# C attention: transposing the probabilities on VectorE and through a scratch array instead of on TensorE

## The chip, the cores and the metric

The kernel runs on one NeuronCore of a Trainium2 chip. Its engines work side by side and meet at semaphores: TensorE (PE in the profile; its weight loads are PEld), VectorE (DVE), ScalarE (ACT), GpSimd (POOL) and SyncE (SP), which here only issues DMAs. The metric is the device time of one execution in microseconds (us).

## The reference, cut to what matters

Two layers over a sequence of 1024 rows of width 2048, in float32. Each layer projects `x` with `w_in`, runs three mixers on parts of the result, gates them, projects with `w_out`, and normalises. The change touches mixer C alone: eight heads of width 64, in chunks of 64 frames, where each frame sees its own chunk and the eight before.

```python
s = jnp.einsum('bnqhd,bnkhd->bnhqk', qc, kb).astype(jnp.float32) * (C_HEAD_DIM ** -0.5)
s = s + bias[None, None]                       # bias[h, clip(t - s)]
s = jnp.where(valid[None, :, None, None, :], s, NEG_INF)
p = jax.nn.softmax(s, axis=-1)
o = jnp.einsum('bnhqk,bnkhd->bnqhd', p.astype(vb.dtype), vb)
```

The scores come out with the queries on the partitions. The last product needs the probabilities `p` with the keys on the partitions, so they must be transposed.

## The kernel before, in words

The work goes in four **steps** (`it` 0 to 3): two layers, and in each the first and the second half of the sequence, 512 rows. A step is even (first half) or odd (second half). Each step has these parts in this order: four **pairs** of C heads (`pair(p)`, which also hold mixer A), a part for keys and values of B (`KV0`), eight tiles of B (`B0`), and the output projection (`O0`). The layer normalisation of a step (`centre`, `gain_and_bias`, `turn_rows`) is done by VectorE inside the pairs of the next step.

All projections are cut into **units**: 512 columns of 128 weight rows, each worth 12 matmuls of 512 columns (fp32 is split into a high and a low part, and three of the four products are kept). A pair holds 24 units. For each unit SyncE loads `raw` (256 KB, ring of four), ScalarE rounds it to `wh` (L974, `split`), GpSimd subtracts to get `wl` (L1340), and TensorE uses both. ScalarE's split of unit u + 3 stands in its program at `slot(u)` and waits until TensorE is done with unit u - 1; SyncE's load of a unit waits until GpSimd has finished with the unit four before it. So a load is issued about seven units ahead of its use.

Inside a pair the scores are made in four **rounds** j = 0 to 3, each for 128 queries of both heads. A round of an odd step sees five blocks of 128 keys (640 columns); a round of an even step sees j + 1 blocks. A round is this chain:

1. `c_scores` (PE): scores into the PSUM bank pair `sc`.
2. `c_max` (DVE, L1422 to L1426): bias added, negated row maximum.
3. `c_exp` (ACT, L1026): exponential into `prob`, with row sums.
4. `c_normalise` (DVE, L1432, L1433): reciprocal, and `prob` times it.
5. `c_transpose` (PE, L681): each 128x128 block by a matmul with the identity, into `sc` again.
6. `c_hi` (ACT) and `c_lo` (DVE, L1373): high and low part of it, from `sc` into `pt`.
7. `c_attend` (PE): values times `pt`, into `pv`. Then `c_low_rows` (ACT) and `c_add` (DVE, L1403, L1406) fold the parts into `c_att`.

Each engine runs its own written order, in which these pieces stand between the units: all four rounds lie between unit 16 and the first unit of the next pair (unit 24), and the chain of one round ends before that of the next is far along. The product with the gate (`attention_product`) and its high and low parts (`mix_hi`, `mix_lo`) close the pair. The pairs are hardware loops (`Fori`) on each engine. The identifiers `tmp`, `values_scratch` and `store_values` belong to the transposing of C's values, which already goes by VectorE's 32x32 transposes and a scratch array in HBM.

Of the kernel before, what the change touches and what calls it, by code (L numbers as in the profile page):

```python
# [54 lines left out]
TWOS = B_TILES // 2  # L55
C_KEYS = 640
# [22 lines left out]
O0 = B0 + B_TILES * U_B  # L79
U_STEP = O0 + 4 * U_N  # L80

# [22 lines left out]
def build(nc, x, x_t, wall, a_gw, a_scale, sinks, rel_rev, ln_gain, ln_bias, rope_cos, rope_sin,  # L104
          pool_coef, pool_inv, out):
    with ExitStack() as ctx:
# [19 lines left out]
        bval_d = nc.dram_tensor("b_values_scratch", (DEPTH, CHUNK + SEQ, P), F32, kind="Internal").ap()  # L126
        tz_d = nc.dram_tensor("bias_rows_scratch", (DEPTH * 8, P * TZ), F32, kind="Internal").ap()
# [20 lines left out]
        bq0 = sb("bq0", [P, CHUNKS, 2, CHUNK], F32R)  # L148
        pt = sb("pt", [P, 5, 2, 2, P], F32R)
# [32 lines left out]


# [58 lines left out]
        c_out = [pv[:, 0:512], pv[:, 512:1024], pv[:, 0:512], sc[0][:, 0:512]]  # L242
# [62 lines left out]
        hist_in = sem("hist_in")  # L305
# [5 lines left out]
        cs_exp = sem("cs_exp")  # L311
        cs_prob = sem("cs_prob")
        ct_full = sem("ct_full")
# [60 lines left out]
        def last_rows(t, a, b):  # L374

            return sums[:, 4 * t:4 * t + 4, :].rearrange("p c n -> p (c n)")[:, a:b]

# [21 lines left out]
        def _(sp):  # L399
# [98 lines left out]
            for it in range(STEPS):  # L498
                with sp.Fori(0, C_PAIRS) as p:
                    for s in range(U_C):  # L500
                        if s == (4 if it else 0):

                            sp.wait_ge(gwl_ok, p + (C_PAIRS * it + 1))
                            sp.dma_start(gw[:], a_gw[layer(it), ds(p, 1)].rearrange("o c d -> (o c) d")
                                         ).then_inc(gw_in, 16)
                        if s == 9 and half(it):

                            sp.wait_ge(w_used, unit(it, p * U_C) + (2 + RING))
                            for m, a, b in ((mixh, 0, 3), (mixl, 3, 6)):
                                sp.dma_start(m[:, MIX_B:MIX_B + 2 * (b - a) - 1:2, :].bitcast(F32),  # L510
                                             hist_d[ds(p, 1), :, a:b, :].rearrange("o p a n -> (o p) a n")
                                             ).then_inc(hist_in, 16)
                        if s == 10:

                            sp.wait_ge(bias_ok, p + (C_PAIRS * it + 1))
                            if it:
                                sp.wait_ge(rope_ok, (B_TILES + 1) * it)
                                sp.wait_ge(bt_full, 2 * B_TILES * it)
                            else:
                                sp.wait_ge(tz_out, p * (16 * DEPTH) + 16 * DEPTH)  # L520
                            sp.dma_start(brope[:, 0, :].rearrange("p (h n) -> p h n", h=2),
                                         tz_d[ds(2 * p + 8 * layer(it), 2), 127:127 + P * (TZ - 1)]
                                         .rearrange("h (q c) -> q h c", c=TZ - 1)[:, :, 0:NEAR]).then_inc(bias_in, 16)
                        if s == 8 and it:

                            sp.wait_ge(w_used, unit(it, p * U_C) + (1 + RING))
                            load_ln(it - 1, p)
                        at = s - (15 if it else 8)
                        if at == 0:
                            store_values(it, p)  # L530
                        if at == 1:
                            load_values(it, p)
                        if s == 20 and it:
                            store_ln(it - 1, p)
                        if s in (21, 22) and turns(it):
                            store_turned(it - 1, p, s - 21)
                            if s == 22:
                                store_turned(it - 1, p, 2)
                        if s == (23 if it else 15) and not half(it):

                            wait_alone(k_ok, p + (C_PAIRS * it + 1))
                            wait_alone(v_ok, p + ((C_PAIRS + 1) * it + 1))
                            for m, a, b in ((mixh, 0, 3), (mixl, 3, 6)):
                                sp.dma_start(hist_d[ds(p, 1), :, a:b, :].rearrange("o p a n -> (o p) a n"),
                                             m[:, MIX_B + 1:MIX_B + 2 * (b - a):2, :].bitcast(F32)).then_inc(hist_out, 16)
# [91 lines left out]
        def _(pe):  # L637
# [98 lines left out]
            for it in range(STEPS):  # L736
# [7 lines left out]
                def pair(p, first=False):  # L744
# [6 lines left out]
                    else:  # L751
                        for s in range(1, 4):
                            quarter(s, 0)
# [1167 lines left out]
```

## Time and profile before

| | |
|---|---|
| median of 3 runs | 2826.12 us (2825.72 to 2827.51) |
| the profiled execution, its own time | 2824.71 us |
| its span in the trace | 2822.9 us |
| granted TensorE clock, mean | 0.999 of full |
| PE, PEld busy | 2807.9 us (99%), 2352.1 us (83%) |
| DVE, ACT, POOL busy | 1762.0 us (62%), 1297.4 us (46%), 1277.3 us (45%) |
| DMA | 384.49 MB, queue q1 44.2% of 16 engines, 311957 packets, of which 129408 under 512 B |

"Busy" is the time in which at least one instruction of the engine runs. Matmuls overlap: one of 512 columns is shown as 390 ns long, and the next starts 0.23 us after it, so the cost of a matmul is read from start to start. An instruction group's line gives busy time and mean length, and behind the bar the engine's idle time before it and what ended that.

### The profile page before, as it was taken

The numbers are of one execution on the slowest core, as the hardware profiler recorded it, in microseconds if no ns is written. First come the engines' busy times: TensorE is split into PE (matmuls) and PEld (weight loads), VectorE is DVE, ScalarE is ACT, GpSimd is POOL, SyncE is SP. The second block draws the span as 40 slices with busy tenths as digits, with TensorE's granted clock in tenths as the row PEclk, the third lists the DMA queues.
The fourth block names the chain that finished last, engine by engine and source line by source line (L and its number), as shares of the span: only waits on it lengthen the run. The fifth ranks groups of instructions, "written<-read, shape, count | busy, mean of one in ns | idle before, by whom it ended". The sixth has DMA issues, their size and how long they took to land.

```text
span 2822.9 us, 45252 instructions
## 1 busy us (share of the span) xinstructions
PE 2807.9 (99%) x13316; PEld 2352.1 (83%) x13316; DVE 1762.0 (62%) x2950; ACT 1297.4 (46%) x2685; POOL 1277.3 (45%) x927
## 2 busy tenths in 40 slices
PE   9999999999999999999999999999999999999998
PEld 7888888888888888888888888888888888888886
DVE  5555679623777777862266666895137766678625
ACT  5444466523444445652244444664235444456521
POOL 4444444444444434444444444444444444444441
PEclk9999999999999999999999999999999999999999
DMA  6444332355555533335565663324564454333442
GB/s 212 132 133 131 100 89 82 112 175 176 169 168 167 162 91 98 86 94 179 172 192 172 174 173 105 86 82 133 155 214 133 129 155 151 100 86 84 136 157 101
DMA packets 311957, 384.49 MB, mean 136 GB/s; under 512 B 129408, under 2 KB 149920, under 8 KB 308128
## 3 DMA queue, kind: packets, MB, share of 16 engines
q1 hardware_dynamic: 308048, 367.26, 44.2%
q10 hardware_dynamic: 3792, 15.73, 1.4%
q8 instruction: 66, 1.08, 0.2%
q14 instruction: 51, 0.42, 0.0%
HBM read 327.23 MB, written 58.81 MB: 137 GB/s over the span
## 4 chain that ended last, share of the span: by engine, by line
PE 99%; DVE 0%; DMA 0%; issue 0%; ACT 0%; POOL 0%; SPq 0%; POOLq 0%
PE acc L639 70%; PE sc L639 18%; PE pv L639 9%; PE sc L681 2%; PE sc L718 1%; DMA raw<-in_wall 0%; DVE last_sums L1840 0%; DVE last_sums L1839 0%; POOL wl L1340 0%; DVE xl L1373 0%; SPq L489 0%; DVE av L1811 0%; DVE last_sums L1820 0%; ACT wh L974 0%; ACT xh L974 0%
## 5 line engine op out<-in xcount | busy, mean ns | idle before, releaser
L1340 POOL TENSOR_TENSOR wl<-raw,wh 128x512 fp32r<-128x512 f32 x920 | 1276.5, 1391 | 1501.9 <-ACT wh L974 1499.9
L974 ACT ACTIVATE wh<-raw 128x512 fp32r<-128x512 f32 x920 | 575.6, 630 | 1053.1 <-PE acc L639 722.3
L639 PE MATMUL acc<-xh,wh 128*128 128x512 f32 x2624 | 1034.0, 394 | 1.2 <-DVE xl L1373 1.2
L639 PE MATMUL acc<-xh,wl 128*128 128x512 f32 x2624 | 1022.7, 390 | 0.0
L639 PE MATMUL acc<-xl,wh 128*128 128x512 f32 x2624 | 1022.6, 390 | 0.0
L639 PEld LDWEIGHTS acc<-xh,wl 128*128 128x128 f32 x2624 | 492.6, 188 | 105.4
L639 PEld LDWEIGHTS acc<-xh,wh 128*128 128x128 f32 x2624 | 493.2, 188 | 98.2 <-DVE xl L1373 2.0
L639 PEld LDWEIGHTS acc<-xl,wh 128*128 128x128 f32 x2624 | 493.6, 188 | 94.0
L1373 DVE TENSOR_TENSOR xl<-prob,xh 128x512 f32 x48 | 55.6, 1158 | 235.8 <-ACT xh L974 235.8
L639 PE MATMUL sc<-wh,mixh 128*128 128x512 f32 x496 | 193.5, 390 | 0.1
L639 PE MATMUL sc<-wl,mixh 128*128 128x512 f32 x496 | 193.0, 389 | 0.0
L639 PE MATMUL sc<-wh,mixl 128*128 128x512 f32 x496 | 193.0, 389 | 0.0
L1373 DVE TENSOR_TENSOR pt<-sc,pt 128x512 fp32r<-128x512 f32 (+3 forms) x192 | 120.1, 663 | 80.7 <-ACT pt L974 79.7
L974 ACT ACTIVATE pt<-sc 128x512 fp32r<-128x512 f32 (+3 forms) x192 | 104.1, 577 | 82.2 <-PE sc L718 43.8
L1026 ACT ACTIVATE prob<-sc,nmax 128x640 f32<-128x640 f32 (+4 forms) x128 | 84.8, 662 | 71.9 <-DVE nmax L1426 70.0
L639 PEld LDWEIGHTS sc<-wh,mixh 128*128 128x128 f32 x496 | 93.1, 188 | 19.6 <-POOL wl L1340 0.5
L639 PEld LDWEIGHTS sc<-wh,mixl 128*128 128x128 f32 x496 | 93.1, 188 | 19.4
L639 PEld LDWEIGHTS sc<-wl,mixh 128*128 128x128 f32 x496 | 93.2, 188 | 19.1
L639 PE MATMUL acc<-wh,mixh 128*128 128x512 f32 x256 | 100.0, 391 | 0.0
L639 PE MATMUL acc<-wh,mixl 128*128 128x512 f32 x256 | 99.7, 389 | 0.0
L639 PE MATMUL acc<-wl,mixh 128*128 128x512 f32 x256 | 99.7, 389 | 0.0
L639 PE MATMUL pv<-wh,mixh 128*128 128x512 f32 x240 | 93.4, 389 | 0.0
(217 smaller groups left out, 3577.4 us busy)
## 6 DMA issues: line engine op xcount, KB each, us to landing
raw<-in_wall SPq DMA_DIRECT2D x920, 256.0 KB, 2.7
res_scratch<-res ACTq DMA_DIRECT2D x12, 1024.0 KB, 4.2
res<-res_scratch SPq DMA_DIRECT2D x12, 1024.0 KB, 4.9
res<-in_x SPq DMA_DIRECT2D x8, 1024.0 KB, 7.3
x_scratch<-res SPq DMA_DIRECT2D x8, 1024.0 KB, 5.2
x_t_scratch<-turned SPq DMA_DIRECT2D x128, 64.0 KB, 2.6
prob<-x_t_scratch SPq DMA_DIRECT2D x32, 256.0 KB, 2.8
res<-x_scratch SPq DMA_DIRECT2D x8, 1024.0 KB, 6.2
```

The source lines that it names most:

```text
L639: return nc.tensor.matmul(o, lhsT, rhs, start=start, stop=stop)
L681: last = nc.tensor.transpose(sc[h][:, cs], prob[:, h, cs], ident[:])
L718: last = nc.tensor.transpose(b_sc[g][:, u, c, :], probs(v, g)[:, u, c, :], ident[:])
L974: return nc.scalar.activation(o, i, ACT.Copy, scale=scale)
L1026: nc.scalar.activation(prob[:, h, c0:C_KEYS], sc[h][:, at:at + C_KEYS - c0], ACT.Exp, bias=nmax[:, h, 0:1], accum_out=psums[:, h, 0:1]).th ...
L1340: nc.gpsimd.tensor_tensor(wl[:, s, :], raw[:, s, :], wh[:, s, :].bitcast(F32), ALU.subtract).then_inc(w_lo, 1)
L1373: return V.tensor_tensor(o, whole, hi.bitcast(F32), ALU.subtract)
```

## The change

The transposing of C's probabilities leaves TensorE. VectorE transposes each 32x32 square of `prob` in place (`V.transpose`), SyncE stores the four bands of 32 rows into `c_prob_scratch` in HBM with the squares put in their new places (four DMAs for each head and round, in pieces of 128 bytes), and loads the transposed blocks back into `pt_raw`, an fp32 view of the place of the low part of `pt` (one DMA for each head and round). `c_hi` and `c_lo` then read `pt_raw` in SBUF instead of `sc` in PSUM. Between the reciprocal and the transpose ScalarE multiplies `prob` by the reciprocal (a `Copy` with a scale), where VectorE did.

The pieces are put in other places of every engine's program. Rounds 0 to 2 get their scores after units 16, 19 and 22, round 3 after unit 1 of the next pair (unit 25); the products with the values come after units 23, 27, 30 and 34. C's closing product (`c_tail_product`, `mix_hi`, `mix_lo`) is between units 11 and 15 of the next pair. The last pair of a step does this in the KV and B parts. `exp` of a round now also waits until the stores of the round before have landed (`cp_out`), since it overwrites `prob`. The load of gain and bias into `prob` waits for the same. The loops over pairs are written out. `hist_in` is split in two, for keys and for values, and the values are loaded later.

```diff
+STORE_AT = (26, 29, 32, 36)
+LOAD_AT = (28, 31, 35, 38)
+ROPE_AT = C_PAIRS * 24 + 11
...
+            def store_c_prob(it, p, j, h):
+                n = c_step(it, p, j)
+                if n:
+                    sp.wait_ge(cp_in[h], 16 * n)
+                sp.wait_ge(cs_prob, 2 * n + h + 1)
+                c0 = 0 if half(it) else 512 - P * j
+                for r in range(4):
+                    rows = slice(32 * r, 32 * (r + 1))
+                    sp.dma_start(cprob_d[h, c0:C_KEYS, rows].rearrange("(m a) b -> a m b", a=32),
+                                 prob[rows, h, c0:C_KEYS].rearrange("a (m b) -> a m b", b=32)).then_inc(cp_out[h], 16)
+
+            def load_c_prob(it, p, j, h):
+                n = c_step(it, p, j)
+                sp.wait_ge(cp_out[h], 64 * (n + 1))
+                if n:
+                    sp.wait_ge(c_pv, n)
+                b0 = 0 if half(it) else 4 - j
+                sp.dma_start(pt_raw[:, b0:5, h, :], cprob_d[h, b0 * P:C_KEYS, :].rearrange("(c k) q -> k c q", k=P)
+                             ).then_inc(cp_in[h], 16)
...
+            def load_gain_bias(it, n):
+                if n:
+                    for h in range(2):
+                        sp.wait_ge(cp_out[h], 64 * c_step(it + 1, n, 0))
...
-            def c_transpose(it, p, j):
-                c0 = 0 if half(it) else 512 - P * j
-                for h in range(2):
-                    pe.wait_ge(cs_prob, p * 8 + (8 * C_PAIRS * it + 2 * j + h + 1))
-                    for b in range(c0 // P, 5):
-                        cs = slice(b * P, (b + 1) * P)
-                        last = nc.tensor.transpose(sc[h][:, cs], prob[:, h, cs], ident[:])
-                    last.then_inc(ct_full, 1)
...
             def c_exp(it, p, j):
...
+                    if n:
+                        act.wait_ge(cp_out[h], 64 * n)
+                    act.wait_ge(cs_max, 2 * n + h + 1)
                     nc.scalar.activation(prob[:, h, c0:C_KEYS], sc[h][:, at:at + C_KEYS - c0], ACT.Exp,
                                          bias=nmax[:, h, 0:1], accum_out=psums[:, h, 0:1]).then_inc(cs_exp, 1)
+                for h in range(2):
+                    act.wait_ge(cs_rinv, 2 * n + h + 1)
+                    copy(prob[:, h, c0:C_KEYS], prob[:, h, c0:C_KEYS], rinv[:, h, 0:1]).then_inc(cs_norm, 1)
...
-                    V_(V.reciprocal(rinv[:, h, 0:1], psums[:, h, 0:1]))
-                    V.tensor_scalar(prob[:, h, c0:C_KEYS], prob[:, h, c0:C_KEYS], rinv[:, h, 0:1], None, ALU.mult
-                                    ).then_inc(cs_prob, 1)
+                    V.reciprocal(rinv[:, h, 0:1], psums[:, h, 0:1]).then_inc(cs_rinv, 1)
+                for h in range(2):
+                    dv.wait_ge(cs_norm, p * 8 + (8 * C_PAIRS * it + 2 * j + h + 1))
+                    V.transpose(prob[:, h, c0:C_KEYS], prob[:, h, c0:C_KEYS]).then_inc(cs_prob, 1)
...
-                    lo(ptl[:, b0:5, h, :], sc[h][:, b0 * P:5 * P].rearrange("p (b q) -> p b q", q=P), pth[:, b0:5, h, :]
-                       ).then_inc(ct_lo, 1)
+                    lo(ptl[:, b0:5, h, :], pt_raw[:, b0:5, h, :], pth[:, b0:5, h, :]).then_inc(ct_lo, 1)
```

On TensorE, an odd step of the kernel before, the end of unit 22 of a pair: the transposes of round 2 stand before mixer A's product (`mixh,bq`), and the scores of round 3 and the values' product of round 2 follow with nothing between them.

```order
L681 MATMUL sc<-ident,prob 128x128 x10
L788 REGISTER_ALU
L639 MATMUL acc<-mixh,bq 128x512
L639 MATMUL acc<-mixl,bq 128x512
...
L639 MATMUL sc<-mixh 128x320 x4
L665 REGISTER_ALU
L639 MATMUL sc<-mixl 128x320 x4
L687 REGISTER_ALU
L639 MATMUL pv<-pt,mixh 128x256 x5
L639 MATMUL pv<-pt,mixl 128x256 x5
```

The same place of the changed kernel, up to the first unit after the next scores:

```order
L699 MATMUL acc<-mixh,bq 128x512
...
L699 MATMUL sc<-mixh 128x320 x4
L699 MATMUL sc<-mixl 128x320 x4
L699 MATMUL acc<-xh,wh 128x512
...
L699 MATMUL pv<-pt,mixh 128x256 x5
L699 MATMUL pv<-pt,mixl 128x256 x5
L699 MATMUL acc<-xh,wh 128x512
...
```

No transposes are left, and one unit's twelve matmuls stand between the scores of round 2 and the values' product, now of round 0.

On VectorE, an odd step of the kernel before, rounds 2 and 3 of a pair:

```order
L1433 TENSOR_SCALAR prob<-prob,rinv 128x640
L1401 REGISTER_ALU
L1403 TENSOR_TENSOR c_low<-pv,c_low 64x512
L1356 REGISTER_ALU
L1406 TENSOR_TENSOR c_att<-c_low 64x128 x2
L1373 TENSOR_TENSOR pt<-sc,pt 128x5x128 x2
L1648 SCALAR_TENSOR_TENSOR tmp<-acc,scale,gate 128x512
L1419 REGISTER_ALU
L1422 MEMSET sc 64x64
```

The same engine in the changed kernel, from `c_lo` of round 0 to `c_lo` of round 1, which is past the end of the pair:

```order
L1455 TENSOR_TENSOR pt<-pt_raw,pt 128x5x128 x2
L1750 SCALAR_TENSOR_TENSOR tmp<-acc,scale,gate 128x512
...
L1518 STREAM_TRANSPOSE prob<-prob 128x640 x2
L1455 TENSOR_TENSOR mixl<-tmp,mixh 128x512
L1485 TENSOR_TENSOR c_low<-pv,c_low 64x512
L1488 TENSOR_TENSOR c_att<-c_low 64x128 x2
L1474 SCALAR_TENSOR_TENSOR gate<-gate,acc 128x512
...
L1509 TENSOR_REDUCE nmax<-sc 128x1
L1455 TENSOR_TENSOR pt<-pt_raw,pt 128x5x128 x2
```

Between the two `c_lo` stand now: A's product, the maxima of round 2 and its transposes, A's low part, a fold, the gate, and the maxima of round 3.

On SyncE, the changed kernel, the end of an odd step's last pair (`raw` are the unit loads):

```order
L430 DMA raw<-in_wall 128x512
L477 DMA c_prob_scratch<-prob 32x20x32 x8
L430 DMA raw<-in_wall 128x512 x3
L487 DMA pt_raw<-c_prob_scratch 128x5x128 x2
L619 DMA brope<-in_rope_cos 128x512
```

Each round puts eight stores and two loads into the queue of the unit loads; the kernel before has none of them.

## Rows read from the trace of the kernel before

**Rows 1.** chain that ended last, of the page: shares of the span by engine.
```profile
PE 99%; DVE 0%; DMA 0%; issue 0%; ACT 0%; POOL 0%; SPq 0%; POOLq 0%
```

**Rows 2.** waits of TensorE over the whole span: us, times, longest.
```profile
PE sc L735 <- POOL ident L1333: 1.6, 1, 1.6
```

**Rows 3.** timeline of TensorE, plain stretch: start us, length us, instruction, count.
```profile
403.25 0.39 PE L639 MATMUL acc<-xh,wh 128*128 128x512 f32 x1
...
405.06 0.39 PE L639 MATMUL acc<-xh,wl 128*128 128x512 f32 x1
```

**Rows 4.** timeline of TensorE, odd step, transposes of five blocks.
```profile
2308.15 1.25 PE L681 MATMUL sc<-ident,prob 128*128 128x128 f32 x10
2309.16 0.48 PE L639 MATMUL acc<-xh,wh 128*128 128x512 f32 x1
...
2310.63 0.76 PE L639 MATMUL sc<-mixh 128*128 128x320 f32 x4
```

**Rows 5.** timeline of TensorE, even step, transposes of one block.
```profile
1606.22 0.38 PE L681 MATMUL sc<-ident,prob 128*128 128x128 f32 x2
1606.36 0.48 PE L639 MATMUL acc<-xh,wh 128*128 128x512 f32 x1
...
1608.50 0.40 PE L639 MATMUL sc<-mixh 128*128 128x256 f32 x2
```

**Rows 6.** instruction group of TensorE: count, busy us, mean ns.
```profile
L681 PE MATMUL sc<-ident,prob 128*128 128x128 f32 x480 | 63.3, 273 | 0.0
```

**Rows 7.** timeline of VectorE, odd step, quarter two.
```profile
2320.57 0.11 DVE L1422 MEMSET sc<- 64x64 f32 x1 [0.38 <-PE sc L639]
...
2322.66 0.82 DVE L1426 TENSOR_REDUCE nmax<-sc 128x1 f32<-128x640 f32 x1
...
2327.50 1.56 DVE L1373 TENSOR_TENSOR pt<-sc,pt 128x640 fp32r<-128x640 f32 x2
2328.97 0.74 DVE L1648 SCALAR_TENSOR_TENSOR tmp<-acc,scale,gate 128x512 f32<-128x512 f32 x1
```

**Rows 8.** timeline of ScalarE, the same stretch.
```profile
2323.55 0.80 ACT L1026 ACTIVATE prob<-sc,nmax 128x640 f32<-128x640 f32 x1
2324.24 0.19 ACT L1026 ACTIVATION_READ_ACCUMULATOR prob<-sc,nmax 128x1 f32 x1
2325.04 0.63 ACT L974 ACTIVATE wh<-raw 128x512 fp32r<-128x512 f32 x1 [0.61 <-PE acc L639]
2326.27 1.30 ACT L974 ACTIVATE pt<-sc 128x640 fp32r<-128x640 f32 x2 [0.60 <-PE sc L681]
```

**Rows 9.** instruction groups of VectorE by form.
```profile
L1373 DVE TENSOR_TENSOR pt<-sc,pt 128x640 fp32r<-128x640 f32 x64 | 49.8, 820 | 26.3 <-ACT pt L974 25.8
L1373 DVE TENSOR_TENSOR mixl<-s,mixh 128x512 fp32r<-128x512 f32 x16 | 20.7, 1294 | 13.2 <-ACT mixh L974 13.1
L1403 DVE TENSOR_TENSOR c_low<-pv,c_low 64x512 f32<-64x512 f32 x48 | 32.6, 679 | 0.5
L1544 DVE STREAM_TRANSPOSE turned<-res 128x512 f32<-128x512 f32 x32 | 19.9, 680 | 0.2
L1406 DVE TENSOR_TENSOR c_att<-c_low 64x128 f32<-64x128 f32 x128 | 71.8, 561 | 3.1
```

**Rows 10.** instruction group of GpSimd, of the page.
```profile
L1340 POOL TENSOR_TENSOR wl<-raw,wh 128x512 fp32r<-128x512 f32 x920 | 1276.5, 1391 | 1501.9 <-ACT wh L974 1499.9
```

**Rows 11.** DMA issues of the page: KB each, median us to landing.
```profile
raw<-in_wall SPq DMA_DIRECT2D x920, 256.0 KB, 2.7
x_t_scratch<-turned SPq DMA_DIRECT2D x128, 64.0 KB, 2.6
```

**Rows 12.** DMAs to the scratch array of values: ns min/median/max, landing.
```profile
L420 SPq DMA_DIRECT2D values_scratch<-tmp x64: 348/355/2172, 37.8 to 2361.4; - x64
DMA to landing us min/median/max: 1.7/2.1/10.0
```

**Rows 13.** busy us of PE, PEld, DVE, ACT, POOL over one odd pair.
```profile
2178.00:2258.30 80.30, 80.30 (x406) 68.29 (x405) 57.04 (x97) 38.29 (x68) 35.72 (x25) 1.00 0.44 141
```

More of the change, by code:

```diff
@@ L79 @@
 O0 = B0 + B_TILES * U_B
+O0_BEGIN = B0 + U_B
 U_STEP = O0 + 4 * U_N
@@ L311, in build @@
         cs_exp = sem("cs_exp")
+        cs_rinv = sem("cs_rinv")
+        cs_norm = sem("cs_norm")
         cs_prob = sem("cs_prob")
-        ct_full = sem("ct_full")
+        cp_out = [sem(f"cp_out{h}") for h in range(2)]
+        cp_in = [sem(f"cp_in{h}") for h in range(2)]
         ct_hi = sem("ct_hi")
@@ L498, in _ @@
             for it in range(STEPS):
[L499 to L545, printed above, removed]
-                        if it == 0:
-                            load_unit(it, p * U_C + (s + FIRST), (s + FIRST) % RING)
-                        else:
-                            load_unit(it, p * U_C + s, s % RING)
-                        if s == 23 and it:
-                            if turns(it):
-                                store_turned(it - 1, p, 3)
-                            wait_alone(ln_out, p * 16 + (64 * (it - 1) + 16))
@@ L751, in pair @@
                     else:
-                        for s in range(1, 4):
-                            quarter(s, 0)
+                        quarter(1, 0)
+                        if p:
+                            c_scores(it, p - 1, 3)
+                        quarter(2, 0)
+                        quarter(3, 0)
+                        if p:
+                            c_attend(it, p - 1, 1)
                         pe.wait_ge(gate_ok, p * 2 + (MIXES * it + 1))
@@ L1112, in pair @@
                     else:
-                        for s in range(2, 5):
-                            slot(s)
+                        slot(2)
+                        if p:
+                            c_hi(it, p - 1, 1)
+                        slot(3)
+                        if p:
+                            c_exp(it, p - 1, 3)
+                        slot(4)
                     used(it, p * U_C + (6 if first else 3))
@@ L1572, in _, with c_tail_product @@
                 pc, nb = C_PAIRS * it, 16 * it
-                per_c = 27 + (2 if it else 0) - half(it)
-                with dv.Fori(0, C_PAIRS) as p:
-                    section(p * per_c + total)
+                def c_tail_product(p, values):
+                    dv.wait_ge(c_fold, c_step(it, p, 3) + 1 + 2)
+                    attention_product(p * 2 + (MIXES * it + 2), values)
+                for p in range(C_PAIRS):
+                    section(total)
+                    if p:
+                        c_max(it, p - 1, 3)
+                        c_lo(it, p - 1, 1)
                     V.tensor_copy(coef1[:], coef[:, ds(p, 1), :].rearrange("p o n -> p (o n)"))
@@ L1660, in _ @@
                     if not half(it):
                         dv.wait_ge(hist_out, p * 32 + (32 * C_PAIRS * layer(it) + 32))
-                    assert count[1] == per_c, (it, count[1])
-                total += C_PAIRS * per_c
+                    total += count[1]
                 section(total)
+                p = C_PAIRS - 1
+                c_max(it, p, 3)
+                c_lo(it, p, 1)
+                c_normalise(it, p, 3)
+                c_add(it, p, 1)
+                c_lo(it, p, 2)
@@ L1667, in _ @@
+                dv.wait_ge(rope_in, 32 * (it + 1))
+                rotate(it, 0, KV0 + 3, 0)
+                c_add(it, p, 2)
+                rotated_query(ROTS * it + 1, 0)
+                rotate(it, 1, KV0 + 7, 1, 1.0)
+                c_lo(it, p, 3)
+                c_add(it, p, 3)
+                c_tail_product(p, C_PAIRS * (it + 1))
                 dv.wait_ge(prod_ok, MIXES * it + 2 * C_PAIRS + 2)
```

288 lines of the change are left out of this document (186 added, 102 removed).

## The prediction

> **What bounds the kernel now.** I read the chain that ended last first: TensorE has 99% of it [rows 1]. Then TensorE's waits: the longest entry of the whole span is 1.6 us, at the start [rows 2]. So TensorE runs without a gap, at full clock (a granted clock of 1.00 in [rows 13]), and the time is the sum of what its instructions cost from start to start. The reader is to see two things in this: anything taken off TensorE is gained in full, and any wait put onto it is lost in full. The other engines have room on average: in an odd pair of 80.3 us VectorE is busy 57.0, ScalarE 38.3, GpSimd 35.7 [rows 13]. Whether they have room at each place is the question of this change.
>
> **What goes.** On a plain stretch nine matmuls start within 1.81 us (403.25 to 405.06), eight intervals, 0.226 us each [rows 3]; a unit of twelve is 2.7 us. The transposes of five blocks and two heads take 2308.15 to 2309.16, 1.01 us; of one block and two heads 1606.22 to 1606.36, 0.14 us [rows 4, 5]. So a further block-and-head costs (1.01 - 0.14) / 8 = 0.109 us. The matmuls behind a run of transposes are late too: six of them take 1.47 us (2309.16 to 2310.63) where 6 x 0.226 is 1.36, and nine take 2.14 (1606.36 to 1608.50) where 2.03 is due, 0.11 us both times. There are 480 transposes [rows 6] in 64 runs (4 steps, 4 pairs, 4 rounds). Sum: 480 x 0.109 = 52.3 us, and 64 x (0.14 - 2 x 0.109 + 0.11) = 2.0 us, together 54.3 us. The busy time of 63.3 us in [rows 6] is not the price, since it counts overlap with the next matmul.
>
> **What TensorE gets.** Scores and values' product were neighbours 48 times and are now apart, each between two projections. A change of form costs at least nothing and at most the 0.11 us seen behind transposes; I take 0.04 us, 2 us in all (0 to 5). The written-out loops cost nothing: TensorE never waited at a loop's end [rows 2], and nothing is added that it must branch for. So without any new wait the profiled time goes from 2824.71 to 2824.7 - 54.3 + 2 = 2772.4 us. The profiled execution is 1.4 us under the median of the runs, and I make the sum against it.
>
> **What the round costs now.** The chain of a round in an odd step, all from rows: maxima of two heads 2.9 us (2320.57 to 2322.66 + 0.82, [rows 7]); the second exponential 0.80 with 0.19 for its sum, a little overlapped, so 0.9 [rows 8]; then new: normalising on ScalarE. No row shows it. Its nearest are the 640-column copies from PSUM, 1.30 for two [rows 8], and the split from SBUF, 0.63 for 512 columns; I take 0.70 each (0.6 to 0.8). The transposes on VectorE: 0.68 us for 128x512 from SBUF to SBUF [rows 9], so 0.85 for 640 columns; the second ends about 0.85 after the second normalise plus a wait for the first. The store: four DMAs of SyncE at 0.355 us each for issuing [rows 12], 2.9 us for two heads, landing 2.6 us after the last of them: 64 KB in 128-byte pieces took a median of 2.6 us, as long as 256 KB of `raw` took in whole rows [rows 11]. Bounds are 1.7 and 10.0 [rows 12]. The load of 320 KB: 2.7 for 256 KB of `raw`, so some 3 to 4 us. From the maxima's end to data in `pt_raw`: 0.9 + 1.4 + 0.9 + 2.9 + 2.6 + 3.5 = 12.2 us, against the 7 to 9 units of 2.7 us (19 to 24 us) that the new places leave between scores and product. The round trip through HBM fits with some 4 us over, after 2.9 us for the maxima.
>
> **What it does to `c_lo`.** Before it read PSUM and took 0.82 us for 640 columns [rows 9]. Now both inputs lie in SBUF. The nearest row is the low part of A's values, 128x512 with both inputs in SBUF: 1.29 us on average [rows 9], near GpSimd's own subtraction of 1.39 [rows 10] rather than near 0.68. So such an instruction often waits for GpSimd's. Bounds for 640 columns are 0.82 and about 1.7; I take 1.15, as GpSimd is busy 35.7 of 80.3 us.
> The Trainium skill ("SBUF — State Buffer", section "SBUF: two separate sides") says why: VectorE with two SBUF inputs and GpSimd share a port pair by an exclusive lock. The trace agrees: 1.29 against 0.68. By that rule the transposes, which have one input, are not held up, and all eight `c_lo` of a pair may be; taken at its worst it gives the second rival below.
>
> **Where it gets tight.** I count from the end of unit 22 in an odd pair, in us. TensorE: scores of round 2 (eight matmuls of 320 columns; by columns and [rows 3] 8 x 0.226 x 320/512 = 1.13, I take 1.25), unit 23, product 0 (ten of 256 columns, 1.13 by the same rule, I take 1.2), unit 24, unit 25, scores 3 (1.25), units 26 and 27: product 1 is due at 17.3. Product 0 is due at 4.0. ScalarE: split 0.63, two `c_hi` 1.4, ready at 2.0. VectorE: `c_lo` 0 ends at 2.9 to 3.8, in time for product 0. Then its queue, in the order shown with the change: A's product 0.74 [rows 7], maxima of round 2 2.9, ending at 6.5 to 7.4; the wait for exponential and normalise and two transposes, to 9.9 to 10.8; A's low part 0.7 to 1.3; the fold, 0.68 and two of 0.29 to 1.3 ([rows 9], mean 0.56; a pair took 1.62 in [rows 7]), the gate, of the same kind as A's product, 0.7: 12.7 to 14.7. Maxima of round 3 (scores are there at 11.9) to 15.6 to 17.6, and `c_lo` 1 to 17.2 to 20.2. Its second half is needed at 17.9. So TensorE waits 0 to 2.3 us there; I take 1.1. There are 8 such places in the two odd steps (three pair boundaries and the KV part, each step): 9 us. Product 3 is due after unit 34, behind `centre`, the transposes of the values and A's low part on VectorE, and its load can only go once product 2 is done (`c_pv`): I take 0.5 us for each of 8 (0 to 1.5), 4 us. At the entry to B, `rotate`, the last folds and the keys' low part now come after C's tail on VectorE: 0.7 us in each step (0 to 2), 3 us. In even steps round 1 has two blocks and round 2 three, every link is shorter, and I take no wait. Together 16 us: 2772.4 + 16 = 2788 us.
>
> **What hides the rest.** A unit's split may be late by three units less split and subtraction, 3 x 2.7 - 0.63 - 1.39 = 6.1 us [rows 3, 8, 10], before TensorE notices. In the odd chain above ScalarE is held for about 4.5 us by the wait for reciprocals; the loads of `raw` are held for 2 to 3 us by ten more issues a round (3.6 us of SyncE) and its waits. Both stay below 6.1, and that is the cover; beyond it each us costs a us. DMA has a mean share of 0.44 in the odd pair [rows 13]; twice 2.6 MB more in 75 us is no new bound, though it makes landings longer.
>
> **Rivals.**
> *No new wait.* If `c_lo` meets GpSimd seldom and folds are short, all lower ends hold: 2772 us. For it: the lower ends above all meet their due times. Against: 32 places must all be in time. Chance 0.2.
> *VectorE late everywhere.* `c_lo`, fold and low parts at their upper ends: 8 x 2.3 + 8 x 1.5 + 4 x 2 = 38 us, 2811 us. For it: 1.29 us against 0.68 for 512 columns [rows 9], and a fold pair of 1.62 [rows 7]. Chance 0.2.
> *The store's landing decides, slower.* `exp` of a round waits until the round before has been stored. In rounds 1 and 3 of an odd pair I find no room there: the store's last DMA is issued about 2.9 us after the transposes and must land within 2.6 us. If a landing in this traffic is 5 to 6 us instead, ScalarE stands with its splits behind it, and the next maxima, `c_lo` and product come about 3 us later, in even pairs as well: 16 x 3.5 + 16 = 72 us, 2844 us. It makes the kernel slower from 52 / 16 = 3.3 us of wait a pair on. For it: landings of up to 10.0 us in [rows 12]; against: medians of 2.1 and 2.6. Chance 0.13.
> The Trainium skill ("DMA: Bandwidth & Descriptors", section "Specifications") speaks for this rival: below 512 bytes a transfer is a read-modify-write and misses line rate, and these pieces are 128 bytes. The trace agrees in part: 64 KB of them take as long as 256 KB in long rows [rows 11]; a wait for it is not in the trace.
> *The removal gives less than it says*, the small switches and waits eat it up to within 0.2%. Chance 0.05.
>
> **How the numbers follow.** My forecast, 2788 us, has 0.42, with its own range of 2779 to 2800. The range given is 2771 to 2822: it takes in the first two rivals and the start of the third, and leaves out the rest of the third. A run tells a difference of 0.2% (5.6 us) from none. Faster by more than that: 0.42 + 0.2 + 0.2 and a little of the third, 0.83. Within it 0.05. Slower 0.12.
>
> **What would show it.** In the changed profile L681's group is gone and the sum of the other TensorE groups is unchanged. TensorE's waits list product 1 of odd steps behind VectorE's `pt` by about 1 us a time, four a step; product 3 and B's first scores behind VectorE by less. `pt` by VectorE takes over 1 us for 640 columns, the transposes of `prob` 0.85, ScalarE's `prob<-prob,rinv` 0.7. The forecast is wrong if unit matmuls wait for GpSimd's `wl` (then a queue was later than 6.1 us), if `exp` waits for the scratch's DMAs by more than 1 us a round, or if even steps wait.

## The result, and the profile after

| | before | after |
|---|---|---|
| median | 2825.96 us (4 runs) | 2915.20 us (4 runs, 2914.46 to 2916.40) |
| the profiled execution's own time, span | 2824.71, 2822.9 us | 2914.46, 2912.4 us |
| granted TensorE clock, mean | 0.999 | 0.984 |

The changed kernel takes 1.0315 of the time before, interval 1.0297 to 1.0333: 89 us slower, where the prediction had 2788 us and a range up to 2822.

The page of the changed kernel: the busy times, what DMA moved, and the chain that ended last by engine.

```profile
PE 2797.6 (96%) x12836; PEld 2323.0 (80%) x12836; DVE 1805.2 (62%) x2950; ACT 1350.6 (46%) x2804; POOL 1276.2 (44%) x927
DMA packets 629705, 448.10 MB, mean 154 GB/s; under 512 B 385664, under 2 KB 467616, under 8 KB 625824
PE 73%; DMA 8%; DVE 8%; SPq 6%; issue 3%; ACT 1%; POOL 1%; ACTq 0%; POOLq 0%; DVEq 0%
```

TensorE lost its 480 transposes (13316 matmuls became 12836) and is no longer the whole chain as in [rows 1]: 22% of it now lies with DMA, VectorE and SyncE's queue. The packets have doubled, and four in five of the added ones are below 512 bytes. TensorE's waits, us in total, times, longest, against [rows 2], where the longest entry is 1.6 us:

```profile
PE pv L699 <- DVE pt L1455: 73.1, 36, 7.6
PE sc L699 <- DVE tmp L1805: 9.8, 4, 3.0
PE sc L699 <- DVE mixh L1467: 6.7, 5, 1.4
PE acc L699 <- DVE mixl L1455: 6.4, 7, 4.2
```

The first is the values' product waiting for the low parts of the probabilities (`c_lo`); "product 2" below is that of round 2. The releaser is VectorE, but VectorE itself waited. (The profile counts a wait from the modelled end of the matmul before, 0.39 us after its start, where the next would have come after 0.227. Where the text sums waits by product or by place, it counts from start to start, 0.16 us more for each.) The group of `c_lo`, by form, and its neighbours, against [rows 7 to 9]:

```profile
L1455 DVE TENSOR_TENSOR pt<-pt_raw,pt 128x640 fp32r<-128x640 f32 x64 | 60.3, 968 | 48.5 <-ACT pt L1031 47.9
L1518 DVE STREAM_TRANSPOSE prob<-prob 128x640 f32<-128x640 f32 x64 | 50.3, 824 | 18.3 <-ACT prob L1031 18.3
L1031 ACT ACTIVATE prob<-prob,rinv 128x640 f32<-128x640 f32 x64 | 49.3, 821 | 1.1 <-DVE rinv L1515 1.1
L1031 ACT ACTIVATE pt<-pt_raw 128x640 fp32r<-128x640 f32 x64 | 45.2, 731 | 60.4 <-DMA pt_raw<-c_prob_scratch 60.1
```

`c_lo` costs 0.97 us (predicted 1.15), the transpose 0.82 (0.85), the normalising on ScalarE 0.82 (0.70). Taken together the work costs about what was predicted. What stands before it does not: VectorE waits for ScalarE's high parts, and those wait for the load from the scratch array. So the chain behind the 73.1 us is read one engine further back, in ScalarE's waits:

```profile
ACT prob L1086 <- DMA c_prob_scratch<-prob: 86.2, 53, 4.9
ACT pt L1031 <- DMA pt_raw<-c_prob_scratch: 75.9, 40, 6.2
ACT wh L1031 <- DMA raw<-in_wall: 68.5, 16, 11.8
```

The last of these in the kernel before:

```profile
ACT wh L974 <- DMA raw<-in_wall: 61.1, 32, 5.0
```

The exponentials wait 53 times for the stores of the round before, the high parts 40 times for the load. The splits' waits for weights are hardly more in sum than before, 68.5 us against 61.1, but the longest has gone from 5.0 to 11.8 us. From the end of a round's maxima to its data in `pt_raw`, averaged over the eight rounds of each number in the odd steps, the trace has 16.1, 18.2, 21.3 and 26.1 us for rounds 0 to 3. The prediction had 12.2. From product 1 of a pair to product 1 of the next, the columns as in [rows 13]:

```profile
812.50:901.20 88.70, 79.50 (x363) 65.64 (x364) 63.71 (x101) 42.11 (x75) 33.94 (x24) 0.96 0.79 199
2255.90:2338.70 82.80, 78.51 (x364) 65.16 (x364) 60.15 (x97) 41.94 (x74) 34.03 (x24) 0.98 0.76 200
```

An odd pair takes 82.8 to 88.7 us instead of 80.3, and DMA's share has gone from 0.44 to between 0.76 and 0.79, for 2.6 MB out and 2.6 MB back.

**The largest waits are in step 0,** three of 7.2 to 7.7 us at product 3 of pairs 0 to 2, though rounds are shorter there. The timeline of ScalarE's queue and ScalarE, and of SyncE's queue, pair 1 of step 0 (start us, length us, instruction):

```profile
180.59 3.52 ACTq L1165 DMA_DIRECT2D bias_rows_scratch<-bias_row_scratch  x2
...
201.90 0.63 ACT L1031 ACTIVATE wh<-raw 128x512 fp32r<-128x512 f32 x1 [11.80 <-DMA raw<-in_wall]
```
```profile
181.10 10.53 SPq L477 DMA_DIRECT2D c_prob_scratch<-prob  x8
191.67 2.70 SPq L430 DMA_DIRECT2D raw<-in_wall  x2
194.47 7.21 SPq L487 DMA_DIRECT2D pt_raw<-c_prob_scratch  x2
```

Issuing eight stores takes 10.5 us instead of the predicted 2.9, and the next weights are issued only behind them. DMA by queue from 182 to 200 us (packets, MB, share of 16 engines):

```profile
q10 hardware_dynamic: 497, 0.76, 11.4%
```

Queue q10 is ScalarE's broadcast of the bias rows, 0.79 MB. 11.4% of sixteen engines is 1.8 engines for 18 us, and the access pattern has two heads as its outer dimension. In the packets of the trace it runs from 182.3 to 200.8 us, never more than two at a time. The last store, issued at 189.4 us, landed at 201.3, half a us after the broadcast's last packet. I take it that the stores' packets for the engines that carry the broadcast stood behind it; the trace does not name the engines, so this is inferred, and e1 tests it. The kernel before had the same broadcast, in 19.8 us from 97.4 us on, but nothing on TensorE's path waited behind it. TensorE in the same place, and what its next matmuls cost:

```profile
197.14 0.39 PE L699 MATMUL acc<-xh,wl 128*128 128x512 f32 x1
205.16 1.19 PE L699 MATMUL pv<-pt,mixh 128*128 128x256 f32 x4 [7.64 <-DVE pt L1455]
206.15 1.05 PE L699 MATMUL pv<-pt,mixl 128*128 128x256 f32 x4
207.01 0.63 PE L699 MATMUL acc<-xh,wh 128*128 128x512 f32 x1
207.43 0.63 PE L699 MATMUL acc<-xl,wh 128*128 128x512 f32 x1
207.86 0.63 PE L699 MATMUL acc<-xh,wl 128*128 128x512 f32 x1
```

After the wait the matmuls of 512 columns start 0.43 us apart, not 0.226: the granted clock fell to 0.5 (1.2 instead of 2.4 GHz). There are 17 such stretches of 3.4 to 11.8 us, the last at the kernel's end, where the kernel before has its only one. 85 intervals between matmuls of 512 columns in them are 0.427 us, 17 us too much. But the products' matmuls of 256 columns stand in them too, and some of 512 are slowed in part. Matmul by matmul against e12 below, whose TensorE program is the same, the 16 stretches cost 29 us on top of the waits, 20 at 512 columns and 9 at 256.

**In the odd steps SyncE's order makes it late.** SyncE's queue in pair 0 of step 1, rounds 2 and 3:

```profile
802.97 0.38 SPq L493 DMA_DIRECT2D res<-res_scratch  x1
805.23 7.65 SPq L477 DMA_DIRECT2D c_prob_scratch<-prob  x8
812.92 1.02 SPq L430 DMA_DIRECT2D raw<-in_wall  x2
814.04 0.38 SPq L556 DMA_DIRECT2D mixh<-hist_scratch  x1
814.46 0.47 SPq L556 DMA_DIRECT2D mixl<-hist_scratch  x1
815.04 0.41 SPq L572 DMA_DIRECT2D brope<-bias_rows_scratch  x1
...
816.05 2.14 SPq L487 DMA_DIRECT2D pt_raw<-c_prob_scratch  x2
818.78 1.50 SPq L430 DMA_DIRECT2D raw<-in_wall  x1
824.38 5.92 SPq L477 DMA_DIRECT2D c_prob_scratch<-prob  x8
```

The stores of round 2 are issued behind 1 MB of residual and take 7.65 us. The load of the round goes behind two history loads and the bias, and its first half lands 8 us after its issue (824.4). The stores of round 3 start exactly then, since the single scratch array must have been read (`cp_in`); round 3's transposes had ended at 817.7 us.

### The profile page after: what moved, and what is told of

It reads as the page before. It is cut to its first block, busy times and chain, and to the rows that moved or that the text cites. A ratio compares the mean times of both kernels' runs of the same rounds, so it can differ in the third digit from the quotient of the medians.

```text
span 2912.4 us, 41599 instructions
## 1 busy us (share of the span) xinstructions
PE 2797.6 (96%) x12836; PEld 2323.0 (80%) x12836; DVE 1805.2 (62%) x2950; ACT 1350.6 (46%) x2804; POOL 1276.2 (44%) x927
## 4 chain that ended last, share of the span: by engine, by line
PE 73%; DMA 8%; DVE 8%; SPq 6%; issue 3%; ACT 1%; POOL 1%; ACTq 0%; POOLq 0%; DVEq 0%
PE acc L699 49%; PE sc L699 15%; PE pv L699 8%; DMA pt_raw<-c_prob_scratch 4%; SPq L477 4%; DMA prob<-in_ln_bias 1%; DVE mixl L1455 1%; DMA c_prob_scratch<-prob 1%; PE sc L768 1%; SPq L430 1%; DVE pt L1455 1%; DMA raw<-in_wall 1%; POOL wl L1422 1%; DVE brope L1719 1%; DVE res L1619 0%
## 5 line engine op out<-in xcount | busy, mean ns | idle before, releaser
L1455 DVE TENSOR_TENSOR pt<-pt_raw,pt 128x640 fp32r<-128x640 f32 (+4 forms) x128 | 106.7, 866 | 93.5 <-ACT pt L1031 92.5
L1031 ACT ACTIVATE pt<-pt_raw 128x640 fp32r<-128x640 f32 (+4 forms) x128 | 72.6, 596 | 85.8 <-DMA pt_raw<-c_prob_scratch 75.9
L699 PE MATMUL pv<-pt,mixh 128*128 128x256 f32 x240 | 45.2, 312 | 69.9 <-DVE pt L1455 69.9
L699 PEld LDWEIGHTS pv<-pt,mixh 128*128 128x128 f32 x240 | 37.7, 207 | 84.5 <-issue 80.6
L1515 DVE RECIPROCAL rinv<-psums 128x1 f32<-128x1 f32 x128 | 20.4, 162 | 131.2 <-ACT prob L1086 130.8
```

Source lines behind the costliest of these rows:

```text
L699: return nc.tensor.matmul(o, lhsT, rhs, start=start, stop=stop)
L1031: return nc.scalar.activation(o, i, ACT.Copy, scale=scale)
L1455: return V.tensor_tensor(o, whole, hi.bitcast(F32), ALU.subtract)
L1515: V.reciprocal(rinv[:, h, 0:1], psums[:, h, 0:1]).then_inc(cs_rinv, 1)
```

## The experiments

Each stands against the kernel before, run on the same chip (medians of 2825.95 to 2826.74 us). All are built on the changed kernel except e8. "us less" is the difference of two medians; the intervals of the ratios are 3 to 6 us to either side.

### e1: bias rows spread over the engines

```diff
-act.dma_start(tz_d[heads].rearrange("h (q c) -> h q c", c=TZ),
-              rel_d[heads].rearrange("h (o c) -> h o c", o=1).to_broadcast([2, P, TZ]))
+act.dma_start(tz_d[heads].rearrange("h (q c) -> q h c", c=TZ),
+              rel_d[heads].rearrange("h (o c) -> o h c", o=1).to_broadcast([P, 2, TZ]))
```

> The changed kernel, with one edit: the bias-row broadcasts on ScalarE's queue have the 128 rows as their outer dimension, not the two heads. Theory A (these DMAs run for 18 us on few of the 16 DMA engines in 1536-byte packets, and round 3's stores of 128-byte pieces wait behind them on those engines): the three waits of 7.6 us before product 3 in step 0 go, 22.8 us, and with them the half-clock stretches behind them, some 4 to 6 us: 2915 to about 2887 us. Rival (the stores are late from traffic as a whole, or from SyncE's issuing): the same bytes move, so step 0 keeps its waits, 2915 us.

Measured: 2877.69 us (2869.65 to 2885.19), ratio 1.0191, interval 1.0174 to 1.0208. That is 37.5 us less. Queue q10 from 163 to 170 us, and TensorE's first wait:

```profile
q10 hardware_dynamic: 540, 0.78, 43.0%
```
```profile
PE pv L699 <- DVE pt L1455: 51.0, 32, 3.4
```

The same bytes pass within 7 us at 43% of the engines instead of 18 us at 11.4%, and the waits of 7 us are gone. It gained more than I expected, since a wait of 4.3 us before unit 16 in step 0 (for the low parts of the keys, which VectorE makes behind the bias) and stretches at half clock went too.

### e8: the same edit in the kernel before

> The kernel before with the bias rows spread over 128 outer rows, as in the first experiment, and nothing else. It has no wait of TensorE on a DMA, so the same edit should give nothing there: 2826 us, within 2 us. If it gains more than that, part of what the edit gave the changed kernel was not the change's to lose.

Measured: 2824.81 us, ratio 0.9995, interval 0.9985 to 1.0004. In the kernel before, the slow broadcast cost nothing. So the 37.5 us belong to the change, as its collision with work that was there. Not all of that collision is with the stores: see the bias rows in e2.

### e2: no round trip

```diff
-    sp.dma_start(cprob_d[h, c0:C_KEYS, rows]..., prob[rows, h, c0:C_KEYS]...)
-    sp.dma_start(pt_raw[:, b0:5, h, :], cprob_d[h, b0 * P:C_KEYS, :]...)
-    copy(pth[:, b0:5, h, :], pt_raw[:, b0:5, h, :])
+    copy(pth[:, b0:5, h, :], <the identity matrix, for each block>)
```

The kernel leaves out the probabilities that are read back, so its output is not the reference's.

> The changed kernel without the scratch round trip: the stores and loads of the probabilities are left out, and c_hi and c_lo read the identity in SBUF instead, after waiting for VectorE's transposes; so the output is not the reference's. Everything on the engines stays. Theory A (the loss is in the DMAs of the trip; VectorE's queue costs what the prediction said, some 1 us at product 1 of odd steps and a few at the entry to B): 2790 to 2810 us. Rival (VectorE's and ScalarE's new orders lose the time even without a DMA): waits before products 2 and 3 stay, over 2860 us.

Measured: 2823.57 us (10 runs), ratio 0.9989, interval 0.9979 to 0.9999. The round trip's DMAs cost 92 us of time. But the result lies between the two expectations: without them the kernel is only as fast as before. TensorE's waits in it:

```profile
PE pv L692 <- DVE pt L1450: 11.7, 18, 0.8
PE acc L692 <- DVE mixl L1450: 10.8, 4, 3.1
PE sc L692 <- DVE tmp L1800: 9.8, 4, 3.0
```

The first line is what the prediction had worked out for `c_lo` at products 1 and 3 (13 us). The second, low keys of step 0 behind the bias rows, and 12 us at half clock were not in it, and the third, at the entry to B, was there with 3 us.

The second line has its far end in the broadcast, with no store in the kernel. VectorE's wait for the bias rows, in e2 and in the kernel before:

```profile
DVE brope L1714 <- DMA brope<-bias_rows_scratch: 43.4, 4, 13.7
DVE brope L1619 <- DMA brope<-bias_rows_scratch: 16.6, 4, 5.1
```

So the slow broadcast reaches TensorE by two ways, the stores behind it and the bias rows that come late from it. e1 cures both, and no run parts its 37.5 us between them.

### e3: history and residual loads moved in SyncE's queue

```diff
-if s == 10 and half(it):        # history keys
+if s == 17 and half(it):
-if s == 8 and it:               # residual
-    sp.wait_ge(w_used, ...)
+if s == (6 if p else 8) and it:
+    if not p: sp.wait_ge(w_used, ...)
```

> The changed kernel with two loads moved in SyncE's queue in no other way than this: the history keys (1 MB) from event 10 to event 17 of a pair, behind round 3's load, and the 1 MB load of the sums to be normalised from event 8 to 6 (pairs 1 to 3). Theory B (a load of the trip waits in the DMA rings behind what SyncE issued just before it; at 816 us it lands 8 us after its issue behind 2 MB): products 2 and 3 of odd steps wait 33 us now and will wait about 10; with the clock stretches 2915 to about 2885 us. Rival (the DMA engines are simply full over the pair, order is no matter): within 5 us of 2915.

Measured: 2891.43 us, ratio 1.0231, interval 1.0214 to 1.0248, 23.8 us less. In the changed kernel pair 1 of step 1 has three waits for `pt`, at products 1 to 3:

```profile
901.21 0.83 PE L699 MATMUL pv<-pt,mixh 128*128 128x256 f32 x5 [1.77 <-DVE pt L1455]
913.77 0.83 PE L699 MATMUL pv<-pt,mixh 128*128 128x256 f32 x5 [1.27 <-DVE pt L1455]
929.52 1.02 PE L699 MATMUL pv<-pt,mixh 128*128 128x256 f32 x5 [3.10 <-DVE pt L1455]
```

Summed over the odd steps, product 2 waits 17.8 us in the changed kernel and not at all in e3. Products 1 and 3 still wait there (1.6 and 2.8 us in the same pair).

### e4: product 1's low parts before the maxima of round 3

```diff
-c_max(it, p - 1, 3)
 c_lo(it, p - 1, 1)
+c_max(it, p - 1, 3)
```

> The changed kernel with c_lo of round 1 before c_max of round 3 on VectorE. Theory C (the wait before product 1 in odd steps is VectorE's queue: the maxima stand before c_lo): the eight waits before product 1, 10.6 us, go, and nothing takes their place, since exp of round 3 waited for the stores of round 2 anyway: about 2902 us with the clock's part. Rival (the delay moves on: maxima, exp and store of round 3 come 2 us later and product 3 waits as much more): 2915 us.

Measured: 2913.69 us, ratio 1.0307, interval 1.0290 to 1.0325: nothing gained. The same pair in e4:

```profile
898.08 0.86 PE L699 MATMUL pv<-pt,mixl 128*128 128x256 f32 x5 [0.25 <-DVE pt L1455]
911.91 1.41 PE L699 MATMUL pv<-pt,mixh 128*128 128x256 f32 x5 [4.80 <-DVE pt L1455]
928.19 0.83 PE L699 MATMUL pv<-pt,mixh 128*128 128x256 f32 x5 [1.37 <-DVE pt L1455]
```

1.77 us at product 1 became 0.25, and 1.27 at product 2 became 4.80. TensorE only came sooner to data that came no sooner: from the landing of round 0's data to that of round 2's it is 30.2 us in the changed kernel and 31.0 in e4. The wait on VectorE's queue that the prediction made its main term was real and not the one that ended last.

### e5, e6, e7: what is left of the landing

e5 is e1 and e3 together.

> Both edits that gained, together: the bias rows spread over 128 outer rows, and history keys and sums moved in SyncE's queue. The first alone gained 37 us (2877.7), the second 24 us (2891.4). If they cure different waits (step 0; product 2 of odd steps), they add: 2854 us. If both only free the same full DMA engines, the second gives less: 2868 us or more.

Measured: 2855.31 us, ratio 1.0113, interval 1.0090 to 1.0135. 59.9 us less than the changed kernel, where 37.5 + 23.8 is 61.3: within the noise the two gains add, so the two causes are apart.

e6 adds a second scratch array, so a round's stores wait for the load of the round before the last:

```diff
-    if n:     sp.wait_ge(cp_in[h], 16 * n)
+    if n > 1: sp.wait_ge(cp_in[h], 16 * (n - 1))
-    cprob_d[h, ...]
+    cprob_d[2 * (n % 2) + h, ...]
```

> The last kernel with a second copy of the scratch array, used in turn by rounds, so that a store need not wait until the load of the round before has landed (36 us of SyncE's waits in 23 places, and the store of round 3 starts at the moment at which round 2's load lands, 824.4 us). Theory D (these waits make round 3's store and load late, and product 3 with them): product 3's waits, 24 us or more, fall by half, 12 to 15 us less than the last kernel. Rival (the load of round 3 also waits for product 2, which frees pt, and this sets the end): 0 to 3 us less.

Measured: 2841.96 us, ratio 1.0057, interval 1.0039 to 1.0075, 13.3 us less than e5.

e7 moves the load of gain and bias behind round 3's load, and the centring waits for the sums alone:

```diff
-dv.wait_ge(ln_in, n * 48 + (192 * it + 48))
+dv.wait_ge(ln_sums_in, 16 * (4 * it + n + 1))
-if s == 13 and it: load_gain_bias(it - 1, p)
+if s == 15 and it: load_gain_bias(it - 1, p)
```

> The last kernel with gain and bias loaded behind round 3's load (event 15, not 13), and VectorE's centring waiting for the sums alone, the product with the gain for gain and bias. Theory E (two 256 KB broadcasts just ahead of round 3's load, and centring that waits for them, delay product 3 in steps 1 to 3): 5 to 8 us less than the last kernel. Rival (the wait moves to the gain, then to the low part of the keys and unit 16): no gain, and waits for the low keys appear.

Measured: 2833.31 us (10 runs), ratio 1.0023, interval 1.0012 to 1.0034, 8.7 us less than e6. The ten executions spread from 2825.25 to 2837.79 us: three lie below 2826 us, the others from 2831 us on. The one with the profile is of the three, so what makes the others longer no trace shows.

### e9, e10, e11: VectorE's order

e9 puts the transpose of the b heads' values before the wait for the last rotated query:

```diff
 rotate(it, 2, B0 + 3, 0)
+V.transpose(tmp[:], v_bank).then_inc(vt_ok, 1)
 rotated_query(ROTS * it + 3, 1)
 sinks_of(it, i)
-V.transpose(tmp[:], v_bank).then_inc(vt_ok, 1)
```

> Base: e7_late_gain. VectorE transposes the new values of the b heads (vt_ok) right after the third rotation, before it waits for ScalarE's high query, instead of after that query's low parts and the copies of the sinks. Theory: the wait at B's first scores (10.5 us in e7, 2.3 to 3.4 us in each of 4 steps) is a wait for VectorE's own queue and goes, nearly all of it, since VectorE stands idle 1.3 us at the new place and TensorE's bank is ready there: e7 minus 9 to 11 us and a few tenths of half clock, so 2820 to 2824. Rival: the scores then wait for ScalarE's query instead (qh_ok and bq_ok lie on the same chain), and no more than 3 us are gained: 2830.

Measured: 2823.47 us (11 runs), ratio 0.9990, interval 0.9981 to 0.9999, 9.8 us less than e7 by the medians, and on another chip. The wait at B's first scores fell from 10.5 to 3.3 us. But the two profiled executions took the same time, 2825.99 us in e7 and 2825.86 in e9, since TensorE's other waits grew by nearly as much: those at the products went from 26.2 to 30.3 us, and all its waits together only from 40.3 to 39.1. So the edit did to its wait what the theory said. That this is where the 9.8 us come from is not shown: e7's seven longer executions make the difference of the medians.

e10 puts `c_lo(3)` before `centre` and `lo(ya_l)`; e11 is e10 with e4's edit.

> Base: e9. VectorE makes product 3's low parts before it centres the residual and before the low part of the shifted values, instead of after both (3.7 us of VectorE's work). Theory: the data of product 3 is there, its low parts stand in VectorE's queue, and the waits at product 3 in steps 1 to 3 (11.9 us in e7, 0.8 to 3.4 us each) go to 2 to 5 us: 8 us less than e9, 2812 to 2816. Rival: the residual's chain (centre, gain, store) is late instead and holds prob and the stores of the next round: no gain or a loss.

> Base: e10. Product 1's low parts before the maxima of round 3 on VectorE, in pair and tail, as e4 did alone on the changed kernel, where the wait only went to product 2. Theory: there SyncE's order of loads made the next stage late, so with that order mended and two scratch buffers the 11.5 us of waits at product 1 go to about 4 and product 2 stays at 3 to 6: 4 to 8 us less than e10, 2805 to 2811. Rival: round 3's chain starts 2.5 us later and product 3 takes the wait over: same as e10 within 2 us.

Measured: e10 2826.41 us (ratio 1.0004, 0.9995 to 1.0013), e11 2831.35 us (1.0021, 1.0011 to 1.0032). Both theories fell. TensorE's waits in e10:

```profile
PE pv L701 <- DVE pt L1457: 17.5, 14, 2.5
PE sc L701 <- DVE mixh L1469: 6.6, 6, 1.2
PE acc L701 <- DVE mixl L1457: 6.2, 9, 1.4
```

The products wait 13 us less than in e9 (30.3 us), and nearly the same 13 us came back where nothing was before: at unit 16 and the scores behind it, for the low keys and low queries, which VectorE now makes later. In e11 product 1's wait went and product 2's came (5.7 us at its first matmuls in step 1). VectorE is busy 63.71 of 88.70 us in the changed kernel's pair above, so it has room on average; but of these two orders each only moved the wait to another place.

### e12: e9 without the round trip

The same identity as in e2 stands for the probabilities that are read back.

> Base: e2_no_trip (no stores and loads of the scratch array; the probabilities read back are left out and the identity stands in their place). Added are the edits of e1 (bias rows spread), e3 (SyncE's order), the centring that waits for the sums alone, and e9 (v's transpose first), all of which showed their worth with the round trip in place. Question: does the time that the removed transposes gave (52 us by the prediction, with the switches) show on the clock once the waits that e2's profile still lists are gone? Theory: yes. e2 had 15 us of waits at weight units (10 to 12 of them at unit 16 of step 0, for low keys behind bias rows), 10 us at B's first scores, 14 us at products 1 and 3, 8 us at half clock; 12 + 9 + 2 + 5 go: 2795, in 2788 to 2803. Rival: the saving isn't there, something else of the step (weights, VectorE's total) fills up to the old time, as e7, e9 and e10 all stand at 2823 to 2833: 2815 or more.

Measured: 2792.21 us (4 runs), ratio 0.9877, interval 0.9861 to 0.9894. Its busy times, its chain and its longest waits:

```profile
PE 2759.1 (99%) x12836; PEld 2302.7 (83%) x12836; DVE 1787.1 (64%) x2950; ACT 1348.7 (48%) x2804; POOL 1272.8 (46%) x927
PE 86%; DVE 10%; issue 2%; ACT 2%; DMA 0%; SPq 0%; POOL 0%; ACTq 0%; DVEq 0%; POOLq 0%
```
```profile
PE pv L694 <- DVE pt L1452: 11.5, 17, 0.8
PE sc L694 <- DVE mixl L1452: 2.6, 2, 1.3
```

The saving is there on the clock. And e12 is 4 us above the predicted 2788: the prediction had described a kernel whose round trip costs nothing, whose bias rows come in time and whose entry to B is mended as in e9. Without these edits the same kernel, e2, takes 31 us more. In its mended form (e9) the trip still costs 2823.5 - 2792.2 = 31.3 us (the two ran on different chips; by the ratios it is 32); as the change had it, 2915.2 - 2823.6 = 91.6 us.

## Why the prediction was wrong

**What goes: right.** With every interval that holds a wait (23 in e12, 2 before) counted as a plain 0.227 us, TensorE's start-to-start times sum to 2755.4 us in e12 and 2807.4 in the kernel before, 52.0 us less. The prediction had 54.3 off and 2 on for changes of form, 52.3.

**What the round costs: this step failed.** It gave 12.2 us from maxima to data, with some 4 us over. The runs show 16.1 to 26.1 in odd steps and 15.7 to 24.8 in even ones. The 4 us were not free either: the high part (0.73 us a head) and `c_lo` (0.97) still stand between the data and the product, some 2.4 us for two heads, and the sum left them out. Term by term, odd steps:

| term | predicted | measured, rounds 0 to 3 |
|---|---|---|
| maxima's end to transposes' end | 3.2 | 5.3, 4.9, 3.5, 5.3 |
| transposes' end to stores landed | 5.5 | 5.7, 8.4, 8.4, 12.4 |
| landed to second load issued | 0 | 0.5, 0.2, 2.6, 1.5 |
| load landing | 3.5 | 4.5, 4.6, 6.8, 7.0 |

The issue of 0.355 us and the landing of 2.6 us were medians of DMAs that ran in a queue with room. Here eight of them stand together, behind weights and residual, and SyncE needs 4.6 to 7.0 us to issue them. The first term is 5.3, 3.3, 3.3 and 4.3 us in e12, where `exp` waits for no store, so part of its excess lies in the engines' own orders (splits that ScalarE does in between); 1.6 us in round 1, 0.2 in round 2 and 1.0 in round 3 came with the trip, where `exp` waits for the stores before. Both bounds stood in the prediction ([rows 12], landings up to 10.0 us and an issue of 2172 ns); it took the median for a path of 64 rounds.

**DMA is no new bound: wrong in kind.** A mean share of 0.44 [rows 13] said nothing of a broadcast that keeps some two engines busy for 18 us, nor of what stands ahead in SyncE's queue. The first cost 37.5 us (e1, e8), the second 23.8 (e3) and 8.7 (e7), the single scratch array 13.3 (e6). From the changed kernel to e9 it is 91.7 us, of the 127 us between forecast and result. Of this the steps to e6, 73.2 us, are clear of the spread; the last 18.5 (e7, e9) are differences of medians of which the seven longer executions of e7 make a part.

**`c_lo` and product 1: right in size, and not what decided.** Predicted 8 waits of 1.1 us; the changed kernel has eight, 10.6 us in sum, e12 has eight of 0.96. e4 shows that mending them alone gains nothing. Product 3 in odd steps: 4 us predicted, 15.0 in the changed kernel, of which e12, without DMA, has 4.6.

**The entry to B: mis-sized.** 0.7 us a step was taken, bound 2; it is 2.0 to 3.2, 10.4 us in the changed kernel. Tail, keys' low part, third rotation, its query and the sinks stand in one line on VectorE, and the prediction had counted only what was added.

**Even steps: wrong.** "Every link is shorter, I take no wait" left out what else is in the queues: 22.8 us at product 3 of step 0 alone, where e1's edit leaves none.

**The cover of 6.1 us: not what failed.** In step 0 a split waited 11.8 us for its weights behind the stores' issue, more than the cover. But TensorE had come to product 3 at 197.5 us and stood there until 205.2, and behind that wait the late split (done at 202.5) no longer showed. In the whole span TensorE waited for `wl` once by more than 0.15 us, 0.5 us in step 0, and never for a split.

**Not foreseen: the clock.** No step of the sum asked what a wait does to the matmuls after it. Of the 29 us that half clock cost in the changed kernel nothing is left in e12.

**The rival that came nearest** was the third: the stores' landing, slower than before, and in even pairs too. Its place was one of several, and its price was too low: 72 us on 2772.4, where 142 came. It had a chance of 0.13; the step that should have made it the likeliest is the one above. What stays open: how the 31.3 us that the trip still costs in e9 divide between `exp`'s wait for the stores and the load's landing; no run parts the two. Open too is why e7's executions differ by up to 12 us.

Of the kernels that compute the whole, none is clearly faster than the one before: e9 stands at 0.9990 (0.9981 to 0.9999), below one but by less than the 0.2% that matters.

## What to carry to other kernels

When work moves from a saturated engine to a round trip through HBM, lay its DMAs into the issuing queue's timeline, with what stands ahead of each, and take the price in that place, not a median of DMAs that nobody waited for. Look for transfers with a small outer dimension: the one here cost nothing until stores had to pass it and its own result was needed sooner. Read a wait back over the engines until one waited for nothing: the three edits that began at its far end (e1, e3, e6) gained 75 us, the one at the engine named (e4) nothing.

## What the runs showed of the hardware

- A broadcast whose outer dimension is 2 kept 1.8 of 16 DMA engines busy for 18 us, never with more than two packets at a time, and stores of another queue issued beside it were issued and landed late; with 128 outside it passed within 7 us at 43% of the engines.
- Eight stores in pieces of 128 bytes took SyncE 4.6 us to issue in the median of the 64 rounds, and 10.53 and 7.65 us in the two places above, where the median DMA to the scratch array of values took 0.355.
- In the changed kernel 16 stretches at a granted clock of 0.5, of 3.4 to 10.2 us, began in or up to 1.5 us after a wait of TensorE, of 1.8 to 7.6 us or two shorter ones close together; matmuls of 512 columns started 0.427 us apart. Not every such wait was followed by one: those of 2.6 and 2.8 us at product 2 in step 3 were not. Half clock cost 29 us there, 8 in e7, 10 in e9 and none in e12, whose waits behind the first are of at most 1.3 us.
- ScalarE's multiply of 640 columns from SBUF by a scale per partition took 0.82 us, its plain copy of the same size 0.73.
